# Sums of gated tiles beside the up rounds: from GpSimd to VectorE, one item ahead

## The chip, the cores and the metric

One NeuronCore of a Trainium2 chip runs the whole program. The metric is device time in microseconds, the median of several runs. TensorE multiplies, ScalarE (ACT), VectorE (DVE) and GpSimd (POOL) compute on tiles, and SyncE (SP) issues nearly all DMAs.

## What is computed

One layer of a hybrid encoder for 2048 prompt rows and 64 sample rows, 1024 wide: two token mixers, an output projection, and a gated feed-forward block with a short causal convolution. The change lies in the feed-forward block:

```python
h = modulate(x, norm_ffn_g[l], shift, scale)
up, cf_new = causal_dwconv(h @ ffn_up_w[l], cf_prev, ffn_conv_w[l], ffn_conv_b[l])
val, gt = jnp.split(up, 2, axis=-1)
x = x + gate[:, None, :] * ((val * jax.nn.gelu(gt)) @ ffn_down_w[l])
```

D_FF is 2816, so there are 22 tiles of 128 hidden channels (`NF`), in 11 pairs (`NI`).

## The kernel before

All engines run programs written out by hand, and semaphores tie them together. Nothing schedules: what stands first on an engine's queue runs first.

**Products with seven terms.** Each large matrix product is cut in 2 x 2 blocks and made from seven block products (Winograd's form of Strassen's scheme) in place of eight. That needs sums and differences of the blocks of both operands. Each operand, a block or a sum of blocks, is split in two f16 parts, high and low, and each product is three passes (high-high, high-low, low-high). ScalarE makes the high part by a copy, VectorE the low part by subtracting the high one.

**The up rounds.** Round f (1 to 21; round 0 stands ahead) multiplies all tokens by the up weights of hidden tile f. TensorE runs seven products `c` in three column groups `q` of 352, 21 blocks of 12 matmuls a round (L2981). ScalarE copies some of them out of PSUM (`copy`, L1751). VectorE combines others (`block`, L2635, L2638, L2641). `block(f, 1, 2)`, L2638 on the last 352 columns, is the last of them. ScalarE's `c21` (L1759 for the first two column groups, L1762 for the third) empties product 6. It stands on ScalarE's queue behind `first_tap(f, 0)` (L1788), which waits for that last `block`. TensorE's next round writes the banks that `c21` empties.

In round f VectorE also does the convolution of tile f - 1 (`ffn_conv`: L2651 and L2655, for the value and then for the gate half), the gated product of tile f - 1 (`product`, L2659), the sums of the next up weights (`weight_sums`, L2612 to L2617) and their low parts (`up_lo`, L2583). ScalarE makes the high parts (`up_hi`, L1713) and the gelu (L1794).

**Items.** The down product that comes after the up rounds needs the seven combinations of the gated hidden tiles as well. For the first eight pairs (`NQ` = 8) these are made beside the up rounds 3 to 18, in a loop of eight passes with two rounds each, `late` = 0 and 1. An item is 176 columns of one pair of tiles, six items a pair, so 48 items (`NITEM`), three a round. For an item, in this order:
- SP loads four blocks of 128x176 f32 from `ffn_hidden` (L942)
- four sums and differences are made in three new tiles and one of the loaded (`four_sums`, L1204 to L1209, on GpSimd)
- ScalarE makes the high parts (`item_hi`, L1810 and L1811)
- VectorE makes the low parts (`item_lo`, L2671 and L2673)
- SP stores all to `hidden_combinations` (L947)

Two sets of buffers for the loaded blocks and the sums are used in turns, one for the result.

**Units** are the same for the down weights: load (L932), four sums on GpSimd (`unit_sums`, L1194 to L1199), high parts (`unit_hi`, L1804, L1805), low parts (`unit_lo`, L2663, L2666), store (L936). There are two a round in the loop.

Where they stand in a round: `item_lo` of the first item behind the value half of the convolution, of the second behind `product`, of the third ahead of `up_lo` of weight 4. GpSimd's queue in a round holds sums of item, item, unit, item, unit. After the up rounds, `base_sums` on GpSimd does the same sums for the last three pairs.

SP's queue in a round: item store, item load, up weights, store of the hidden tile f - 1, item store, item load, unit store, unit load, item store, item load, unit store, unit load. Ahead of the loop it loads items 0 and 1.

Of the kernel before, what the change touches and what calls it, by code (L numbers as in the profile page):

```python
# [12 lines left out]
ALU = mybir.AluOpType  # L13
# [50 lines left out]
def build(nc, a):  # L64
    ctx = ExitStack()
    with ctx:
# [537 lines left out]
        LOAD_BASE = 8 * (NITEM + 2)  # L604
        SUM_BASE, HI_BASE, LO_BASE = 4 * NITEM, 2 * NITEM, 2 * NITEM + 6

# [516 lines left out]
        def _(pool):  # L1123
# [86 lines left out]

            def item_sums(n, i, u):
                pool.wait_ge(b_loaded[u % 2], 48 * i + 16 * (u // 2) + 16)
                pool.wait_ge(b_lo, 2 * n + 4)
                four_sums([itemr[u % 2][:, k] for k in range(4)], [isum[u % 2][:, k] for k in range(3)], 4 * n)

            def loop_sums(i, late):
                (n0, _, _), (n1, _, _), (n2, _, _) = loop_items(i, late)
                u0, u1 = loop_units(i, late)
                item_sums(n0, i, 3 * late)
                item_sums(n1, i, 3 * late + 1)  # L1220
                unit_sums(u0)
                item_sums(n2, i, 3 * late + 2)
                unit_sums(u1)
# [10 lines left out]

            def base_sums(s):
                if s == NB - 1:
                    pool.wait_ge(b_last, LAST_BASE + 16)
                else:
                    pool.wait_ge(b_loaded[s % 2], loads_done(s))
                if s >= 2:  # L1240
                    pool.wait_ge(b_lo, LO_BASE + 2 * (s - 1))
                four_sums([stage_of(s)[:, :, k] for k in range(4)], [dsum[s % 2][:, :, k] for k in range(3)],
                          SUM_BASE + 4 * s)
# [738 lines left out]
        def _(dve):  # L1982
# [678 lines left out]
            def unit_lo(n):  # L2661
# [5 lines left out]
                    .then_inc(wu_lo, 1)  # L2667

            def item_lo(n, i, u):
                dve.wait_ge(b_hi, 2 * n + 1)  # L2670
                dve.tensor_tensor(iout[:, 0:4, 1], itemr[u % 2], iout[:, 0:4, 0], ALU.subtract).then_inc(b_lo, 1)  # L2671
                dve.wait_ge(b_hi, 2 * n + 2)
                dve.tensor_tensor(iout[:, 4:7, 1], isum[u % 2], iout[:, 4:7, 0], ALU.subtract).then_inc(b_lo, 1)  # L2673

            def base_lo(s):
# [74 lines left out]
            ffn_round(1, units_of(1))  # L2750
            ffn_round(2, units_of(2))
            with nc.vector.Fori(0, LOOPS) as i:
                ffn_round(round_a(i), loop_units(i, 0), loop_items(i, 0))
                ffn_round(round_a(i) + 1, loop_units(i, 1), loop_items(i, 1))
# [589 lines left out]
```

## Time and profile before

| what | value |
|---|---|
| median of 3 runs | 2704.09 us (2703.27 to 2707.04) |
| the profiled execution | 2708.34 us, its span 2706.2 us |
| TensorE busy | 2645.6 us, 98% of the span |
| VectorE busy | 1750.4 us, 65% |
| ScalarE busy | 1361.6 us, 50% |
| GpSimd busy | 622.1 us, 23% |
| clock of TensorE that was granted | 0.993 of full speed |

The span is the time from the first to the last instruction of one execution. A row of a timeline gives the start and the length in us, the engine, the line, the operation with its output and input, the number of operations merged in it, and in brackets how long the engine stood idle before it and what ended that. An engine starts its next operation up to 0.1 us before the end that is shown of the one before, so the distance from start to start is what counts.

### The profile page before, as it was taken

What the parts mean: (1) busy time and instruction counts of PE and PEld (TensorE: products, weight loads), DVE (VectorE), ACT (ScalarE), POOL (GpSimd) and SP (SyncE); (2) the same over time, 40 slices, a digit from 0 to 9 for tenths busy, and PEclk for the clock granted to TensorE, in tenths of its full rate; (3) what the DMA queues carried; (4) which work ended last, traced back from release to release, by engine and by line L of the source; (5) the groups of instructions that cost most, each with busy time, mean ns of one, the idle gap of its engine ahead of it and who ended that gap; (6) DMA issues with size and microseconds to landing.
All of it is one profiled execution on the core that took longest, in us unless ns stands there. A gap on an engine that the chain in (4) does not pass through costs nothing.

```text
span 2706.2 us, 50623 instructions
## 1 busy us (share of the span) xinstructions
PE 2645.6 (98%) x18662; PEld 1771.9 (65%) x18662; DVE 1750.4 (65%) x3369; ACT 1361.6 (50%) x2666; POOL 622.1 (23%) x697
## 2 busy tenths in 40 slices
PE   8998999999999999999999999999999999999997
PEld 2465666666668888556997666666666666666664
DVE  4965374564746665767777788888888875242434
ACT  4966474655756665113556455565555653121211
POOL 2600000000008789000000245443344311101000
PEclk9999999999999999999999999999999999999999
DMA  8622212231183543456652354545545438566562
GB/s 280 201 71 98 102 62 71 70 111 69 62 234 96 123 143 126 174 215 189 149 142 64 125 183 167 182 163 184 181 159 182 164 122 327 206 238 253 221 249 91
DMA packets 238419, 423.07 MB, mean 156 GB/s; under 512 B 57816, under 2 KB 162776, under 8 KB 230056
## 3 DMA queue, kind: packets, MB, share of 16 engines
q1 hardware_dynamic: 229400, 412.03, 45.5%
q10 hardware_dynamic: 8848, 8.74, 0.9%
q8 instruction: 109, 1.79, 0.3%
q14 instruction: 62, 0.51, 0.1%
HBM read 283.42 MB, written 139.92 MB: 156 GB/s over the span
## 4 chain that ended last, share of the span: by engine, by line
PE 83%; DVE 5%; ACT 5%; DMA 2%; issue 2%; POOL 1%; SPq 1%; DVEq 0%; ACTq 0%; POOLq 0%
PE ps L2981 52%; PE ps L3228 14%; PE ps L3087 5%; PE ps L3073 4%; PE ps L3060 3%; PE ps L3049 2%; PE ps L2905 1%; ACT arena L1591 1%; DMA arena<-in_w_down 1%; PE ps L3022 1%; POOL arena L1137 1%; ACT arena L1598 1%; ACT arena L1272 1%; ACT arena L1306 1%; DMA gates<-arena 0%
## 5 line engine op out<-in xcount | busy, mean ns | idle before, releaser
L2981 PE MATMUL ps<-arena 128*128 128x352 f16 (+1 forms) x11880 | 1612.7, 298 | 6.2 <-ACT arena L1759 2.9
L2981 PEld LDWEIGHTS ps<-arena 128*128 128x128 f16 x11880 | 1102.2, 97 | 512.4 <-ACT arena L1759 3.6
L3228 PE MATMUL ps<-arena 128*128 128x352 f16 x2772 | 414.8, 311 | 0.5 <-DVE arena L2680 0.5
L3228 PEld LDWEIGHTS ps<-arena 128*128 128x128 f16 x2772 | 265.5, 96 | 149.9 <-issue 1.0
L1194 POOL TENSOR_TENSOR arena<-arena 128x128 f32<-128x128 f32 x44 | 30.7, 698 | 744.3 <-DMA arena<-in_w_down 744.2
L3087 PE MATMUL ps<-arena 128*128 128x424 f16 (+1 forms) x960 | 174.1, 343 | 3.4 <-DVE arena L2462 2.7
L1150 POOL CAST arena<-arena 64x512 f16<-64x512 f32 x8 | 4.9, 608 | 699.1 <-DMA arena<-in_cache_kT 698.9
L1751 ACT ACTIVATE arena<-ps 128x352 f32<-128x352 f32 x264 | 115.8, 459 | 95.0 <-PE ps L2981 95.0
L3073 PE MATMUL ps<-arena 128*128 128x64 f32 (+2 forms) x1200 | 148.8, 269 | 0.5 <-DVE arena L2426 0.5
L3087 PEld LDWEIGHTS ps<-arena 128*128 128x128 f16 x960 | 92.4, 97 | 84.8 <-DVE arena L2462 4.3
L1204 POOL TENSOR_TENSOR arena<-arena 128x176 f32<-128x176 f32 (+1 forms) x57 | 55.9, 981 | 399.6 <-DMA arena<-ffn_hidden 399.6
L3073 PEld LDWEIGHTS ps<-arena 128*128 128x128 f32 (+2 forms) x1200 | 142.5, 190 | 2.7 <-issue 0.8
L1389 ACT ACTIVATE arena<-ps 128x352 f32<-128x352 f32 x192 | 80.8, 462 | 122.1 <-PE ps L2981 122.1
L2783 DVE TENSOR_TENSOR arena<-ps,arena 128x352 f32<-128x352 f32 x12 | 6.3, 525 | 206.3 <-PE ps L3228 176.4
L2583 DVE SCALAR_TENSOR_TENSOR arena<-arena 128x512 f16<-128x512 f32 x154 | 104.7, 711 | 47.3 <-ACT arena L1713 47.3
L2651 DVE SCALAR_TENSOR_TENSOR arena<-arena 128x2114 f32<-128x2114 f32 x44 | 110.0, 2500 | 27.2 <-ACT arena L1788 27.2
L1598 ACT ACTIVATE arena<-ps 128x512 f32<-128x512 f32 (+3 forms) x136 | 76.2, 561 | 99.1 <-PE ps L3060 99.0
L1178 POOL TENSOR_TENSOR arena<-arena 128x1024 f32<-128x1024 f32 (+6 forms) x147 | 120.4, 819 | 13.6 <-POOL arena L1171 3.8
L2150 DVE SCALAR_TENSOR_TENSOR arena<-arena 128x512 f16<-128x512 f32 x112 | 73.9, 687 | 63.6 <-ACT arena L1368 63.4
L1944 ACT ACTIVATE arena<-ps 128x352 f32<-128x352 f32 x12 | 5.6, 463 | 205.7 <-PE ps L3228 205.7
L1788 ACT ACTIVATE arena<-arena 128x2114 f32<-128x2114 f32 x44 | 94.5, 2147 | 28.3 <-DVE arena L2638 27.3
L2655 DVE SCALAR_TENSOR_TENSOR arena<-arena 128x2114 f32<-128x2114 f32 x44 | 108.2, 2460 | 0.3
(236 smaller groups left out, 3580.1 us busy)
## 6 DMA issues: line engine op xcount, KB each, us to landing
hidden_combinations<-arena SPq DMA_DIRECT2D x48, 616.0 KB, 3.2
arena<-hidden_combinations SPq DMA_DIRECT2D x24, 1232.0 KB, 7.1
arena<-in_w_up SPq DMA_DIRECT2D x44, 512.0 KB, 4.8
down_combinations<-arena SPq DMA_DIRECT2D x44, 448.0 KB, 2.8
ffn_hidden<-arena SPq DMA_DIRECT2D x44, 440.0 KB, 3.1
arena<-down_combinations SPq DMA_DIRECT2D x10, 1792.0 KB, 7.7
arena<-down_combinations SPq DMA_DIRECT2D x20, 896.0 KB, 6.5
arena<-ffn_hidden SPq DMA_DIRECT2D x50, 352.0 KB, 3.9
```

The source lines that it names most:

```text
L1178: pool.tensor_tensor(out, djunk[:, :, 0:w], djunk[:, :, w:2 * w], ALU.add).then_inc(ada_step, 1)
L1598: act.activation(pt[:, x.h, 0:m * P], ps[:, 4, 0:m * P], ACT.Copy).then_inc(t_act, 1)
L1751: act.activation(fcp[(0, 1, 2, 0)[i]][q], ps[:, bank_of((0, 2, 3, 4)[i], q), 0:CF], ACT.Copy, scale=CSF)\
L1788: act.activation(out, u[:, 0:LF], ACT.Identity, scale=w0, bias=fb).then_inc(f_tap, 1)
L2583: dve.scalar_tensor_tensor(fsp[:, c, :, 1, :], src.rearrange("p (k m) -> p k m", k=4), -WSF if c == 6 else WSF, fsp[:, c, :, 0, :], ALU.mu ...
L2651: dve.scalar_tensor_tensor(out, u[:, 1:1 + LF], tap(1), out, ALU.mult, ALU.add).then_inc(f_conv, 1)
L2655: dve.scalar_tensor_tensor(out, u[:, 2:2 + LF], tap(2), out, ALU.mult, ALU.add).then_inc(f_conv, 1)
L2981: mm = pe.matmul(out, wt[:, k, wp, :], act_t[:, k, hp], start=(first and k == 0 and n == 0), stop=(last and k == K - 1 and n == 2), skip_g ...
L3060: mm = pe.transpose(ps[0:k, 4 + c // 4, (c % 4) * P:(c % 4) * P + x.rows], pr[0:x.rows, x.h, c * P:c * P + k], ident[0:x.rows, 0:x.rows])
L3073: mm = pe.matmul(ps[0:x.rows, 6, 64 * x.h:64 * x.h + 64], pt[0:k, x.h, c * P:c * P + x.rows], vv[x.b][0:k, x.v0 + c, 64 * x.h:64 * x.h + 6 ...
L3087: mm = pe.matmul(out, wt[:, wp, k, :], mixT[:, k, hp, t:t + w], start=(k == k0 and m == 0), stop=(k == k1 - 1 and m == 2))
L3228: mm = pe.matmul(ps[:, down_bank(n, k), 0:CF].rearrange("p (w t) -> p w t", w=2), dwt(i)[:, wi, wp, :], dact[i][:, :, bi, hp, :], start=(i ...
```

## The change

The four sums of an item are taken off GpSimd's queue and made by VectorE, with the same semaphore `b_sum`. VectorE makes the sums of item n + 1 directly behind `item_lo` of item n, and those of item 0 ahead of the loop. The last pass makes one set that nobody uses (item 48, for which a load stood there already), so the later counts of `b_sum` grow by four. GpSimd keeps the unit sums and `base_sums`.

```diff
-        SUM_BASE, HI_BASE, LO_BASE = 4 * NITEM, 2 * NITEM, 2 * NITEM + 6
+        SUM_BASE, HI_BASE, LO_BASE = 4 * NITEM + 4, 2 * NITEM, 2 * NITEM + 6
...
-            def item_sums(n, i, u):
-                pool.wait_ge(b_loaded[u % 2], 48 * i + 16 * (u // 2) + 16)
-                pool.wait_ge(b_lo, 2 * n + 4)
-                four_sums([itemr[u % 2][:, k] for k in range(4)], [isum[u % 2][:, k] for k in range(3)], 4 * n)
-
             def loop_sums(i, late):
-                (n0, _, _), (n1, _, _), (n2, _, _) = loop_items(i, late)
                 u0, u1 = loop_units(i, late)
-                item_sums(n0, i, 3 * late)
-                item_sums(n1, i, 3 * late + 1)
                 unit_sums(u0)
-                item_sums(n2, i, 3 * late + 2)
                 unit_sums(u1)
...
             def base_sums(s):
+                if s == 0:
+                    pool.wait_ge(b_sum, SUM_BASE)
...
+            def four_sums(blocks, sums, at0):
+                b12, b11, b22, b21 = blocks
+                t0, t2, t3 = sums
+                dve.tensor_tensor(t0, b12, b11, ALU.subtract).then_inc(b_sum, 1)
+                dve.wait_ge(b_sum, at0 + 1)
+                dve.tensor_tensor(b12, b22, b12, ALU.subtract).then_inc(b_sum, 1)
+                dve.tensor_tensor(t2, b22, t0, ALU.subtract).then_inc(b_sum, 1)
+                dve.wait_ge(b_sum, at0 + 3)
+                dve.tensor_tensor(t3, b21, t2, ALU.subtract).then_inc(b_sum, 1)
+
+            def item_sums(n, i, u):
+                dve.wait_ge(b_loaded[u % 2], 48 * i + 16 * (u // 2) + 16)
+                dve.wait_ge(b_lo, 2 * n + 4)
+                four_sums([itemr[u % 2][:, k] for k in range(4)], [isum[u % 2][:, k] for k in range(3)], 4 * n)
+
             def item_lo(n, i, u):
...
                 dve.tensor_tensor(iout[:, 4:7, 1], isum[u % 2], iout[:, 4:7, 0], ALU.subtract).then_inc(b_lo, 1)
+                item_sums(n + 1, i + (u + 1) // 6, (u + 1) % 6)
...
             ffn_round(2, units_of(2))
+            item_sums(0, 0, 0)
             with nc.vector.Fori(0, LOOPS) as i:
```

The functions moved down by some lines, so the same operation has another line number after: L2663 and L2666 (unit low parts) are L2656 and L2659, L2651 is L2644, L2671 and L2673 are L2679 and L2681.

VectorE's queue at the entrance of the loop, before. The unit's low parts end round 2, and the convolution opens round 3:

```order
L2663 SCALAR_TENSOR_TENSOR arena<-arena 128x4x128 [waits wu_hi]
L2666 SCALAR_TENSOR_TENSOR arena<-arena 128x3x128 [waits wu_hi]
L2752 UNCONDITIONAL_BRANCH
L2752 ISA
L2651 ISA [waits f_tap]
L2651 SCALAR_TENSOR_TENSOR arena<-arena 128x2114
```

The same place after:

```order
L2656 SCALAR_TENSOR_TENSOR arena<-arena 128x4x128 [waits wu_hi]
L2659 SCALAR_TENSOR_TENSOR arena<-arena 128x3x128 [waits wu_hi]
L2665 TENSOR_TENSOR arena<-arena 128x176 [waits b_lo,b_loaded0]
L2667 TENSOR_TENSOR arena<-arena 128x176 [waits b_sum]
L2668 TENSOR_TENSOR arena<-arena 128x176
L2670 TENSOR_TENSOR arena<-arena 128x176 [waits b_sum]
L2762 UNCONDITIONAL_BRANCH
L2762 ISA
L2644 ISA [waits f_tap]
L2644 SCALAR_TENSOR_TENSOR arena<-arena 128x2114
```

The sums of item 0, with their wait for the load, stand ahead of the loop and of the convolution now.

VectorE's queue in round 3 behind the first item's low parts, before, up to the low part of the up weights (L2583):

```order
L2670 ISA
L2671 TENSOR_TENSOR arena<-arena 128x4x176 [waits b_hi]
L2672 REGISTER_ALU
L2673 TENSOR_TENSOR arena<-arena 128x3x176 [waits b_hi]
L2582 ISA
L2583 SCALAR_TENSOR_TENSOR arena<-arena 128x4x128 [waits p_hi]
```

The same place after:

```order
L2678 ISA
L2679 TENSOR_TENSOR arena<-arena 128x4x176 [waits b_hi]
L2680 REGISTER_ALU
L2681 TENSOR_TENSOR arena<-arena 128x3x176 [waits b_hi]
L2673 ISA
L2674 ISA [waits b_loaded1]
L2665 TENSOR_TENSOR arena<-arena 128x176 [waits b_lo]
```

Between the low parts of an item and the next work of the round stand a wait for the next item's load and four operations. The other two items of a round have the same piece.

## Rows read from the trace of the kernel before

**Rows 1.** The page: busy time of the engines; DMA issues, count, size, us to landing.
```profile
PE 2645.6 (98%) x18662; PEld 1771.9 (65%) x18662; DVE 1750.4 (65%) x3369; ACT 1361.6 (50%) x2666; POOL 622.1 (23%) x697
...
arena<-ffn_hidden SPq DMA_DIRECT2D x50, 352.0 KB, 3.9
```

**Rows 2.** Timeline of TensorE, the up rounds: start, length, line, count, idle before.
```profile
1519.27 75.36 PE L2981 MATMUL ps<-arena 128*128 128x352 f16 x504 [2.14 <-ACT arena L1759]
1595.34 676.79 PE L2981 MATMUL ps<-arena 128*128 128x352 f16 x4536 [0.71 <-ACT arena L1759]
```

**Rows 3.** Timeline of all engines, one steady round, 1824 to 1857 us.
```profile
1825.39 0.89 DVE L2671 TENSOR_TENSOR arena<-arena 128x704 f16<-128x704 f32 x1 [1.18 <-ACT arena L1810]
...
1830.60 2.42 DVE L2655 SCALAR_TENSOR_TENSOR arena<-arena 128x2114 f32<-128x2114 f32 x1
...
1835.14 2.36 DVE L2659 SCALAR_TENSOR_TENSOR arena<-arena 128x2114 f32<-128x2114 f32 x1 [0.42 <-ACT arena L1794]
...
1843.16 0.35 SPq L942 DMA_DIRECT2D arena<-ffn_hidden  x1
...
1845.45 0.69 DVE L2583 SCALAR_TENSOR_TENSOR arena<-arena 128x512 f16<-128x512 f32 x1 [0.99 <-ACT arena L1713]
...
1849.03 0.69 DVE L2583 SCALAR_TENSOR_TENSOR arena<-arena 128x512 f16<-128x512 f32 x1 [1.39 <-ACT arena L1713]
...
1851.52 0.52 DVE L2638 SCALAR_TENSOR_TENSOR arena<-ps,arena 128x352 f32<-128x352 f32 x1 [0.23 <-PE ps L2981]
...
1853.31 0.59 DVE L2638 SCALAR_TENSOR_TENSOR arena<-ps,arena 128x320 f32<-128x320 f32 x2 [0.38 <-PE ps L2981]
...
1854.16 2.15 ACT L1788 ACTIVATE arena<-arena 128x2114 f32<-128x2114 f32 x1 [1.48 <-DVE arena L2638]
...
1856.21 0.44 ACT L1759 ACTIVATE arena<-ps 128x352 f32<-128x352 f32 x1
```

**Rows 4.** Groups by line and shape, 1595 to 2150 us: count | busy us, mean ns | idle before.
```profile
L1204 POOL TENSOR_TENSOR arena<-arena 128x176 f32<-128x176 f32 x44 | 42.8, 973 | 92.0 <-DMA arena<-ffn_hidden 92.0
...
L1207 POOL TENSOR_TENSOR arena<-arena 128x176 f32<-128x176 f32 x44 | 26.3, 598 | 0.0
```

**Rows 5.** Timeline of VectorE, a chain of three dependent operations ahead of the up rounds.
```profile
1425.63 0.53 DVE L2540 TENSOR_TENSOR arena<-arena 128x352 f32<-128x352 f32 x1
1426.19 0.34 DVE L2542 TENSOR_TENSOR arena<-arena 128x176 f32<-128x176 f32 x1
1426.45 0.52 DVE L2530 SCALAR_TENSOR_TENSOR arena<-ps,arena 128x144 f32<-128x144 f32 x2
```

**Rows 6.** Timeline of all engines, round 3, the first of the loop, 1555 to 1596 us.
```profile
1555.97 2.42 DVE L2651 SCALAR_TENSOR_TENSOR arena<-arena 128x2114 f32<-128x2114 f32 x1 [1.43 <-ACT arena L1788]
...
1559.78 1.60 POOL L1204 TENSOR_TENSOR arena<-arena 128x176 f32<-128x176 f32 x1 [7.16 <-DMA arena<-ffn_hidden]
...
1564.03 1.05 DVE L2671 TENSOR_TENSOR arena<-arena 128x704 f16<-128x704 f32 x1 [3.06 <-ACT arena L1810]
...
1570.62 2.41 DVE L2655 SCALAR_TENSOR_TENSOR arena<-arena 128x2114 f32<-128x2114 f32 x1
...
1575.15 2.71 DVE L2659 SCALAR_TENSOR_TENSOR arena<-arena 128x2114 f32<-128x2114 f32 x1 [0.43 <-ACT arena L1794]
1575.22 0.44 ACT L1751 ACTIVATE arena<-ps 128x352 f32<-128x352 f32 x1
...
1586.68 0.89 DVE L2671 TENSOR_TENSOR arena<-arena 128x704 f16<-128x704 f32 x1 [1.25 <-ACT arena L1810]
...
1588.43 0.69 DVE L2583 SCALAR_TENSOR_TENSOR arena<-arena 128x512 f16<-128x512 f32 x1 [0.24 <-ACT arena L1713]
...
1591.79 0.58 DVE L2638 SCALAR_TENSOR_TENSOR arena<-ps,arena 128x320 f32<-128x320 f32 x2
...
1592.80 2.13 ACT L1788 ACTIVATE arena<-arena 128x2114 f32<-128x2114 f32 x1
...
1594.84 0.79 ACT L1759 ACTIVATE arena<-ps 128x352 f32<-128x352 f32 x2
```

## The prediction

> **What bounds the kernel now.** I read first the table of engines: TensorE is busy for 98% of the span [rows 1]. So a change on other engines can only cost or give back time where TensorE waits. The second view is therefore TensorE's own timeline through the up rounds [rows 2]. It has two waits there. One is 2.14 us at 1519.27, before round 2 and ahead of the changed loop. The other is 0.71 us at 1595.34, at the start of round 4. After it stand 4536 matmuls in one piece of 676.79 us, 18 rounds of 37.6 us, with no wait at all. Both waits were ended by L1759 on ScalarE. That is `c21`, which empties the first bank of a round's last product. TensorE's next round writes the same bank. So this is the link that ends last, and the question is how near it is to being late in the other rounds.
>
> The third view is one steady round [rows 3]. Round 11 begins on TensorE at 1595.34 + 7 x 37.6 = 1858.5, round 10 at 1820.9. Read the chain ahead of the boundary at 1858.5 backwards: L1759 on ScalarE starts at 1856.21 and ends at 1856.65. It follows the first tap (L1788, 1854.16, 2.15 us), which waited 1.48 us for VectorE's last block (L2638, 1853.31, two pieces, 0.59 us). That block had itself waited 0.38 us for TensorE. The bank is free at 1856.65 and wanted at 1858.47: **a margin of 1.82 us in each round**. VectorE may reach its last block 1.8 us late, and TensorE sees nothing.
>
> **The change, part by part.** GpSimd loses four TENSOR_TENSORs per item, 48 items. Its rows run from 973 ns (L1204) to 598 ns (L1207) for the same shape [rows 4]. Nobody on the path waited for them in the steady rounds: the unit sums that remain on GpSimd wait for a DMA, not for the item sums. So the removal itself gives TensorE nothing.
>
> VectorE gains the four, once per item, behind that item's low halves and for the item after it. Price: the same shape on VectorE is L2542, 128x176 f32, 0.34 us [rows 5]. Where it waits for the operation before it, it starts 0.03 us after that one's end (1425.63 + 0.53 to 1426.19). Where nothing binds the next one, that starts 0.26 us after it (1426.19 to 1426.45). Of the four, two wait for a sum before them. So an item costs 0.37 + 0.26 + 0.37 + 0.26 = **1.26 us**, and three items a round 3.78 us. The bounds: 4 x 0.26 = 1.04 us if no wait is felt, and GpSimd's own price, at least 4 x 0.60 = 2.4 us, if the waits and register instructions cost there what they cost on GpSimd. I take 1.26, as engine and shape are those of the row.
>
> The Trainium skill, "VectorE: DVE Perf Modes", section on the TRN2 errata, gives (N+151)/0.96 ns for such an operation, an estimate of 341 ns that the row bears out, and advises tiles of 512 elements or more, since a small one pays the fixed part alone. By it four serial operations are 1.36 us, and the lateness below would be 1.1 in place of 0.8 us.
>
> In the **steady rounds** the 3.78 us fall between the item's low halves at 1825.39, which ScalarE paces (VectorE waited 1.18 us for it there), and the last block at 1853.31. On that way VectorE waited 0.99 us (1845.45), 1.39 (1849.03), 0.23 (1851.52) and 0.38 (1853.31): 2.99 us that added work can fill. The waits of 0.42 us and less behind a gelu or its own conv stay, since they move with the work. The last block comes 3.78 - 2.99 = **0.79 us late**, the margin falls from 1.82 to about 1.0 us, and TensorE still doesn't wait. The lateness doesn't grow from round to round, for at the next round's item VectorE has another wait for ScalarE (1.18 us at 1825.39) that takes it up. Relief from GpSimd's absence on top is small here, so I count none.
>
> Two waits are new on VectorE. Sums of the item after next wait for its load (`b_loaded`). Behind that wait stand the split of weight 4, the blocks and the last block, and for these wait ScalarE and TensorE. The latest load is issued at 1843.16 [rows 3] and takes 3.9 us [rows 1], so it lands at 1847.1, and some 1.3 us later once the product before it has moved. VectorE was through with the low halves before it at 1849.03 - 1.39 = 1847.64, and would come to it at 1847.64 + 2 x 1.26 - 0.99 = 1849.2. The load lands 0.8 us ahead of need, and a miss of up to 1.0 us is still inside the margin. The wait on `b_lo` is on VectorE's own work of two items back.
>
> At the **entrance of the loop** there is no such cover. VectorE now makes the sums of item 0 ahead of round 3, and the load lands for GpSimd only at 1559.78 [rows 6]. GpSimd waited 7.16 us for it. VectorE had begun its first conv at 1555.97. Now everything behind the sums on VectorE's queue waits with them. Step by step, as lateness against before:
> - first conv: 1559.78 + 1.26 - 1555.97 = +5.07
> - low halves of item 0: the 3.06 us wait at 1564.03 is filled: +2.01
> - second conv, second half (1570.62): one item's sums (+1.26). But VectorE took 6.59 us from 1564.03 to there with GpSimd beside it, against 5.21 in the steady round (1825.39 to 1830.60), so 1.38 come back: +1.89
> - product: 2.71 us before against 2.36 in steady rounds: its end +1.54
> - one more item: +2.80; the wait of 1.25 at 1586.68 is filled, and ScalarE behind the later store is 1.54 late itself: +1.55
> - one more item +2.81, the wait of 0.24 at 1588.43 filled: +2.57 at the last block (1591.79)
> - the first tap on ScalarE began 0.43 us after the block's end, against 0.26 in the steady round, so 0.17 are absorbed: **+2.4** for L1759 and so for TensorE, which was waiting for it already.
>
> Round 4 so begins at 1597.7 in place of 1595.34. Inside round 3 the nearest other need is ScalarE's copy at 1575.22, ending 1575.66. TensorE wants it at 1595.34 - 0.71 - 37.6 + 12 x 1.79 = 1578.5 (twelve of 21 blocks), and +1.9 leaves 0.9 us. From round 4 on the tap ends 0.4 us before the boundary, a conv of 4.9 us later is 4.5 us behind it, and 1825.39 is also 4.5 us behind its boundary: the steady state holds at once.
>
> **The Trainium skill speaks of a lock.** The rows first: beside GpSimd the stretch of 5.21 us took 6.59. "SBUF — State Buffer", section on the two separate sides, says that VectorE and GpSimd share a port pair, and that the one who comes second "fully blocks". By it the relief could be larger than what I counted. What that gives is the second rival.
>
> **Sum.** The profiled execution took 2708.34 us, 4.25 above the median of the three runs. I go by differences: nothing removed from TensorE's path, +2.4 us at one boundary, nothing in the 15 rounds behind it, nothing after the loop, where the operations are the same. 2704.09 + 2.4 = **2706.5 us**.
>
> **Rivals.**
> 1. *VectorE overruns every round (slower).* The margin of 1.82 is crossed when three items cost over 2.99 + 1.82 = 4.81 us, 1.60 us an item. At 2.0 us an item, between my price and GpSimd's 2.4, each boundary is 3 x 0.40 = 1.2 us late, times 15 boundaries 18 us, and the entrance 2.4 + 4 x 0.74 = 5.4: 2727 us. For it: two more waits per item and their register instructions, which no row of VectorE shows in a row of four. Against it: the 0.03 us at the dependent operation. 0.11.
> 2. *Nothing is lost, or the 0.71 us comes back.* If item 0 is absorbed by relief from GpSimd, the wait at 1595.34 goes at most: 2703.4 us. It needs 3.1 us more relief than the rows show. This is also the outcome if the port lock rule above holds for every operation of round 3. 0.10.
> 3. *Two stalls at the entrance.* If the first load is 1 us later (landings spread), round 3 itself stops at the copy, and the total is 3 to 6 us: 2708 to 2710. 0.12, inside the range.
> 4. *A true gain.* TensorE waits 0.71 us in the whole of the changed loop, so over 5.4 us can't come from it. 0.02.
>
> **How the numbers follow.** The forecast gets 0.65. The bounds of its price, 1.04 and about 1.6 us an item, put four items at the entrance at -0.9 and +1.4 us, so it covers 2705.5 to 2708. With the second and third rival and the 3.8 us by which runs of the kernel before differ, the range is 2702.5 to 2710.5, and the first rival is left out. Around 0.2%, 5.4 us, is what a measurement can tell from no change here: faster 0.02, within 0.86, slower 0.12.
>
> **What the profile after would show.** TensorE's timeline has its wait at the start of round 4 grown from 0.7 to about 3 us, and one piece of 18 rounds of 37.6 us behind it. VectorE's first sum waits some 5 us for `ffn_hidden` before round 3. In steady rounds the waits of 0.99 and 1.39 us ahead of the weight splits of product 3 and 4 are gone or nearly so, and L1759 ends 0.8 us nearer to the boundary. A sum of 176 columns takes 0.34 us. I am wrong if TensorE waits for ScalarE or VectorE at more than one boundary, if an item takes over 1.6 us, or if the sums wait for a load in steady rounds by over 1 us.

## The result, and the profile after

The changed kernel took 2716.36 us (median of 7 runs, 2710.93 to 2718.64), the kernel before 2708.01 us (7 runs, 2703.27 to 2712.43). The ratio is 1.0025, 95% interval [1.0014, 1.0036]: slower, and outside the predicted range. Run again later (the first experiment), the same kernel stood at 1.0014 [1.0004, 1.0023]. Neither interval holds 1, and the two ratios put the loss at 6.8 and 3.8 us.

The page after: the engines, and the up products (line, matmuls, busy us and mean ns, idle us before them with the releaser). They answer [rows 1].

```profile
PE 2649.7 (98%) x18662; PEld 1772.7 (65%) x18662; DVE 1793.0 (66%) x3565; ACT 1360.5 (50%) x2666; POOL 481.2 (18%) x505
...
L2991 PE MATMUL ps<-arena 128*128 128x352 f16 (+1 forms) x11880 | 1613.9, 298 | 10.4 <-ACT arena L1752 7.2
```

Work went from GpSimd (141 us less) to VectorE (43 us more, for 196 instructions). TensorE has the same 18662 matmuls, and 7.2 us of its idle time were ended by L1752. That is `c21`, L1759 before. Other lines have moved too: L1781 is the first tap (L1788), L1803 the high half of an item (L1810), L2576 `up_lo` (L2583), L2631 the last `block` (L2638), L2652 `product` (L2659), L2665 to L2670 the sums, now on VectorE.

TensorE's timeline after, the up rounds, against [rows 2]:

```profile
1520.94 75.35 PE L2991 MATMUL ps<-arena 128*128 128x352 f16 x504 [2.08 <-ACT arena L1752]
1601.38 678.31 PE L2991 MATMUL ps<-arena 128*128 128x352 f16 x4536 [5.09 <-ACT arena L1752]
2279.53 31.50 PE L3238 MATMUL ps<-arena 128*128 128x352 f16 x210
```

The whole difference can be read here. The wait at round 4 has grown from 0.71 to 5.09 us. The 4536 matmuls behind it are in one piece again, with no wait at any of the 17 later boundaries, but the piece is 1.52 us longer (678.31 against 676.79). The two windows of TensorE behind that wait say why (window, its length, TensorE busy, granted clock as a share of full speed):

```profile
1601.40:1604.80 3.40, 3.40 (x13) 0.54 0.40 120
1604.80:1638.00 33.20, 33.20 (x225) 1.00 0.52 176
```

In the first window behind the 5.09 us wait TensorE ran at 0.54 of full speed, that is mostly at its lower level, 1.2 GHz, and in the second at 2.4 GHz again. In the profile before, no such stretch follows the 0.71 us wait.

**The measure used from here on.** The time of a whole run can't carry a difference of 3 us from one profile. In the twelve profiles of this study, round 2 of the up rounds starts anywhere from 1517.62 to 1530.06 us, and no kernel changes anything ahead of it. So I take the distance from the start of round 2 to the first down product, which holds all that the change touches in the up rounds. (Behind it the two kernels took 434.2 and 434.4 us.) Before it is 752.70 us (1519.27 to 2271.97, which is where the piece of [rows 2] is followed by the down product). After it is 2279.53 - 1520.94 = 758.59 us: 5.89 us more, 4.37 for the later start of round 4 and 1.52 for the clock. The spans differ by 7.7 us (2713.9 against 2706.2); 1.67 us of that lie ahead of round 2.

**A steady round after**, round 10, against [rows 3]. Its end on TensorE is 1601.38 + 1.52 + 7 x 37.6 = 1866.1.

```profile
1830.03 2.66 POOL L1196 TENSOR_TENSOR arena<-arena 128x128 f32<-128x128 f32 x1
...
1832.96 0.89 DVE L2679 TENSOR_TENSOR arena<-arena 128x704 f16<-128x704 f32 x1 [0.59 <-ACT arena L1803]
...
1852.26 0.35 SPq L942 DMA_DIRECT2D arena<-ffn_hidden  x1
...
1856.74 0.34 DVE L2665 TENSOR_TENSOR arena<-arena 128x176 f32<-128x176 f32 x1
...
1858.26 0.96 DVE L2576 SCALAR_TENSOR_TENSOR arena<-arena 128x512 f16<-128x512 f32 x1
...
1861.64 0.58 DVE L2631 SCALAR_TENSOR_TENSOR arena<-ps,arena 128x320 f32<-128x320 f32 x2
...
1862.47 2.15 ACT L1781 ACTIVATE arena<-arena 128x2114 f32<-128x2114 f32 x1 [1.17 <-DVE arena L2631]
...
1864.53 0.80 ACT L1752 ACTIVATE arena<-ps 128x352 f32<-128x352 f32 x2
```

VectorE's waits of 0.99, 1.39, 0.23 and 0.38 us ahead of its last block are gone. The bank is free at 1864.53 + 0.44 = 1864.97 and wanted at 1866.1, a margin of 1.1 us, where it was 1.82. A load issued at 1852.26 is used at 1856.74, and VectorE doesn't wait for it. The price of a sum, by groups of line and shape from 1602 to 2150 us (count | busy us, mean ns | idle before):

```profile
L2670 DVE TENSOR_TENSOR arena<-arena 128x176 f32<-128x176 f32 x44 | 17.5, 398 | 1.5
...
L2665 DVE TENSOR_TENSOR arena<-arena 128x176 f32<-128x176 f32 x44 | 14.9, 339 | 0.0
```

**The entrance of the loop after**, round 3, against [rows 6]:

```profile
1561.14 0.57 DVE L2665 TENSOR_TENSOR arena<-arena 128x176 f32<-128x176 f32 x1 [5.22 <-DMA arena<-ffn_hidden]
...
1562.74 2.42 DVE L2644 SCALAR_TENSOR_TENSOR arena<-arena 128x2114 f32<-128x2114 f32 x1
...
1567.66 0.89 DVE L2679 TENSOR_TENSOR arena<-arena 128x704 f16<-128x704 f32 x1
...
1574.12 2.42 DVE L2648 SCALAR_TENSOR_TENSOR arena<-arena 128x2114 f32<-128x2114 f32 x1
...
1578.67 2.36 DVE L2652 SCALAR_TENSOR_TENSOR arena<-arena 128x2114 f32<-128x2114 f32 x1 [0.42 <-ACT arena L1787]
...
1586.06 0.33 SPq L947 DMA_DIRECT2D hidden_combinations<-arena  x1
...
1590.65 0.79 ACT L1803 ACTIVATE arena<-arena 128x704 f16<-128x704 f32 x1 [3.48 <-DMA hidden_combinations<-arena]
...
1591.47 0.89 DVE L2679 TENSOR_TENSOR arena<-arena 128x704 f16<-128x704 f32 x1 [1.63 <-ACT arena L1803]
...
1592.90 0.34 DVE L2665 TENSOR_TENSOR arena<-arena 128x176 f32<-128x176 f32 x1
...
1593.25 0.45 POOL L1194 TENSOR_TENSOR arena<-arena 128x128 f32<-128x128 f32 x1 [31.73 <-DMA arena<-in_w_down]
1593.27 0.63 DVE L2667 TENSOR_TENSOR arena<-arena 128x176 f32<-128x176 f32 x1
...
1594.87 0.96 DVE L2576 SCALAR_TENSOR_TENSOR arena<-arena 128x512 f16<-128x512 f32 x1
...
1597.99 0.58 DVE L2631 SCALAR_TENSOR_TENSOR arena<-ps,arena 128x320 f32<-128x320 f32 x2
...
1600.88 0.80 ACT L1752 ACTIVATE arena<-ps 128x352 f32<-128x352 f32 x2
```

Read it from the top. VectorE stands 5.22 us for the load of item 0 with the convolution behind it. It makes that up in part by the third row, the low halves of item 0, since a wait for ScalarE that stood there before (3.06 us) is filled. From 1586.06 on a second loss appears. The store of item 1 is issued there, and only when it has landed may ScalarE overwrite the result tile with item 2 (1590.65). VectorE waits for that, and then makes the next sums while GpSimd makes its unit sums.

### The profile page after: what moved, and what is told of

Its sections match the earlier page's. It is cut to its first block, busy times and chain, and to the rows that moved or that the text cites. A ratio compares the mean times of both kernels' runs of the same rounds, so it can differ in the third digit from the quotient of the medians.

```text
span 2713.9 us, 50637 instructions
## 1 busy us (share of the span) xinstructions
PE 2649.7 (98%) x18662; PEld 1772.7 (65%) x18662; DVE 1793.0 (66%) x3565; ACT 1360.5 (50%) x2666; POOL 481.2 (18%) x505
## 4 chain that ended last, share of the span: by engine, by line
PE 82%; DVE 5%; ACT 5%; DMA 3%; issue 2%; POOL 1%; SPq 1%; DVEq 0%; ACTq 0%; POOLq 0%
PE ps L2991 52%; PE ps L3238 14%; PE ps L3097 4%; PE ps L3083 4%; PE ps L3070 3%; PE ps L3059 2%; PE ps L2915 1%; ACT arena L1584 1%; PE ps L3032 1%; DMA arena<-in_w_down 1%; POOL arena L1137 1%; ACT arena L1265 1%; ACT arena L1591 1%; ACT arena L1299 1%; DMA gates<-arena 0%
## 5 line engine op out<-in xcount | busy, mean ns | idle before, releaser
L1194 POOL TENSOR_TENSOR arena<-arena 128x128 f32<-128x128 f32 x44 | 23.3, 529 | 997.6 <-DMA arena<-in_w_down 997.6
L2644 DVE SCALAR_TENSOR_TENSOR arena<-arena 128x2114 f32<-128x2114 f32 x44 | 107.0, 2431 | 32.9 <-ACT arena L1781 32.9
L1787 ACT ACTIVATE arena<-arena 128x1057 f32<-128x1057 f32 x44 | 45.3, 1076 | 146.7 <-DVE arena L2648 146.7
L2576 DVE SCALAR_TENSOR_TENSOR arena<-arena 128x512 f16<-128x512 f32 x154 | 105.7, 726 | 14.5 <-ACT arena L1706 14.5
L1781 ACT ACTIVATE arena<-arena 128x2114 f32<-128x2114 f32 x44 | 94.5, 2147 | 22.4 <-DVE arena L2631 22.1
```

What stands on the lines that cost most here:

```text
L1781: act.activation(out, u[:, 0:LF], ACT.Identity, scale=w0, bias=fb).then_inc(f_tap, 1)
L2576: dve.scalar_tensor_tensor(fsp[:, c, :, 1, :], src.rearrange("p (k m) -> p k m", k=4), -WSF if c == 6 else WSF, fsp[:, c, :, 0, :], ALU.mu ...
L2644: dve.scalar_tensor_tensor(out, u[:, 1:1 + LF], tap(1), out, ALU.mult, ALU.add).then_inc(f_conv, 1)
```

## The experiments

Three theories stood against each other. (1) The entrance: VectorE starts round 3 some 5 us late behind the load of item 0, TensorE waits for that at round 4 and gets a lower clock for a moment behind the wait. (2) Chance: a long landing of a store, or of the clock, in one execution. (3) Steady overload: VectorE has more to do in each round than it can hide.

The first four ran on one chip and share one set of runs of the kernel before (33 runs, median 2709.98 us); the next four share another (25 runs, 2710.64), the last two a third (23 runs, 2710.84); these six ran on one chip too, another one. "Late" means: counted from the start of round 2, later than the same operation of the kernel before.

**The changed kernel again.** No edit.

> The changed kernel once more, on the chip of the variants below. Theory 1 (entrance): TensorE's timeline again has one long wait in the loop, 4 to 5.5 us at the start of round 4, its clock at half for the first 10 or so matmuls behind it, and 18 rounds of 37.59 us; time over the kernel before by 5 to 7 us. Theory 2 (the long landing of the store in round 3, 4.5 us against 3.2 us before, was chance): the wait is 3 to 4 us this time and the time 3 to 5 us over. Theory 3 (steady overload): waits at several boundaries.

Measured: 2712.0 us (2709.82 to 2716.82), ratio 1.0014 [1.0004, 1.0023]. TensorE's timeline:

```profile
1518.46 77.03 PE L2991 MATMUL ps<-arena 128*128 128x352 f16 x504 [2.09 <-ACT arena L1752]
1597.80 676.79 PE L2991 MATMUL ps<-arena 128*128 128x352 f16 x4536 [2.30 <-ACT arena L1752]
2274.43 55.82 PE L3238 MATMUL ps<-arena 128*128 128x352 f16 x373
```

755.97 us from round 2 to the down product, 3.27 more than before. The lower clock came here at the start of round 2 (504 matmuls in 77.03 us against 75.36). TensorE loses nothing by it directly, since round 4 must wait for `c21` anyway: 0.71 + 3.27 - 1.68 = 2.30, the wait that stands there. The wait came out shorter than either theory had it, and the 3.27 us, like the 3.8 us of the ratio, are what was expected of theory 2. So the loss at the entrance is a mark of the kernel, and its size varies. The long landing of the store and the clock behind the wait belong to the first profile: the store of item 1 landed in 3.5 us here, against 4.5 us there. The entrance itself was later here, though. The load of item 0 was issued 36.70 us after the start of round 2, against 35.92 us in the first profile. Whether the lower clock in round 2 did that is not shown.

**Item 0 alone back on GpSimd**, the other 47 on VectorE:

```diff
+            pool.wait_ge(b_loaded[0], 16)
+            pool.wait_ge(b_lo, 4)
+            four_sums([itemr[0][:, k] for k in range(4)], [isum[0][:, k] for k in range(3)], 0)
             with nc.gpsimd.Fori(0, LOOPS) as i:
...
-            item_sums(0, 0, 0)
             with nc.vector.Fori(0, LOOPS) as i:
```

> The changed kernel, but the sums of item 0 alone are made by GpSimd ahead of the loop, so VectorE waits for no load before round 3; it still makes the other 47 items' sums and one more. Theory 1 (the entrance makes the loss): the first conv of round 3 starts where it did in the kernel before, the wait at round 4 is 0.7 to 2 us, the clock stays full behind it, time 0 to 2 us over the kernel before. Theory 3 (VectorE's load in each round makes the loss): the wait at round 4 may shrink, but the time stays 5 us or more over the kernel before.

Measured: 2712.42 us, ratio 1.0007 [0.9997, 1.0016].

```profile
1525.56 77.03 PE L2993 MATMUL ps<-arena 128*128 128x352 f16 x504 [2.01 <-ACT arena L1755]
1602.85 676.79 PE L2993 MATMUL ps<-arena 128*128 128x352 f16 x4536 [0.27 <-ACT arena L1755]
```

The wait at round 4 is 0.27 us, and 753.92 us pass to the down product (at 2279.48). The lower clock at round 2 makes TensorE 1.67 us later there, and the wait at round 4 is 0.44 us shorter than before: 752.70 + 1.67 - 0.44 = 753.93. Two readings fit this sum. `c21` comes 1.2 us later than before (1602.36 against 1594.84, with round 2 at 1525.56 against 1519.27), so some of these 1.2 us may be the price of the other items at the entrance, hidden here behind the clock, and some of it the clock's. The first convolution of round 3 is 0.4 us late already, ahead of any sum on VectorE. What the run shows is that item 0 makes the greater part of the loss (3.27 or 5.89 us with it), and that the other 47 leave at most 1.2 us. The runs with the loads behind unit 5, below, settle the rest. In whole runs the difference to the changed kernel, 0.0007, is smaller than the intervals; the reading rests on the timeline.

**Both loads earlier, in the changed kernel and in the kernel before.** SP issues the loads of items 0 and 1 in round 2, directly behind the stores of hidden tile 1:

```diff
                     if n == units_of(f)[0]:
                         store_hidden(f - 1)
+                        if f == 2:
+                            item_load(0, 0, 0)
+                            item_load(1, 0, 1)
...
-            item_load(0, 0, 0)
-            item_load(1, 0, 1)
             with nc.sync.Fori(0, LOOPS) as i:
```

> The changed kernel, but SyncE issues the loads of items 0 and 1 in round 2 right behind the store of hidden tile 1, some 7 us earlier, so the data are there when VectorE comes to the sums of item 0. VectorE still makes all sums. Theory 1: VectorE's wait of 5 us is gone, the first conv starts within 0.5 us of the kernel before, low halves of item 0 start 2 us earlier than in the kernel before, and the wait at round 4 is 0 to 0.7 us: time 0 to 1 us below the kernel before. Theory 3: 3 us or more above it.

> The kernel before with the same early loads of items 0 and 1. GpSimd makes the sums of items 0 and 1 while VectorE ends round 2, so VectorE's wait of 3.06 us for the high halves of item 0 falls to about 0.6 us and round 3 ends earlier: the wait of 0.71 us at round 4 goes, time 0.7 us below the kernel before, which this measurement can't tell from none. If it is the same as e2, where the sums are made doesn't matter once the load is early.

Measured: 2711.53 us, 1.0006 [0.9996, 1.0016] with the sums on VectorE, and 2709.83 us, 1.0005 [0.9996, 1.0014] with GpSimd's. To the down product 754.16 and 754.06 us, 1.7 us of each the lower clock behind the wait at round 2. The loads landed 10 us sooner, and the two kernels agree within 0.1 us, so the early load takes the difference between them away. But the gain that was expected on top did not come: the first convolution of round 3 was not back in its place. In the first of them, on GpSimd:

```profile
1560.42 0.45 POOL L1195 TENSOR_TENSOR arena<-arena 128x128 f32<-128x128 f32 x1 [8.02 <-DMA arena<-in_w_down]
```

The item loads wait for the landing of the hidden tile's store. SP stands there, and the unit's store and load are queued behind. ScalarE's first tap, which stands behind the unit's high parts, came 2.1 us later in the one and 2.5 us in the other than in the two runs above. I put that down to SP standing still, but this is the smaller part. The load of unit 5 was issued only 0.6 us later than with item 0 on GpSimd (28.60 us after the start of round 2, against 27.97). What made the difference is its landing, behind two item loads of 352 KB issued just ahead. DMA issues for a window around it, here and in the next version, where it goes ahead of them:

```profile
arena<-in_w_down SPq DMA_DIRECT2D x1, 256.0 KB, 5.3
```

```profile
arena<-in_w_down SPq DMA_DIRECT2D x1, 256.0 KB, 3.1
```

It took 5.7 us in the kernel before with the early loads, and 3.1 us with item 0 on GpSimd.

**Loads behind the load of unit 5.** The same edit, but one unit later in round 2, so that the load of unit 5 goes ahead of the item loads (the store of unit 5 and the load of unit 6 follow them):

```diff
                         unit_load(n + 1)
+                    if f == 2 and n == units_of(f)[1]:
+                        item_load(0, 0, 0)
+                        item_load(1, 0, 1)
```

> The changed kernel with the loads of items 0 and 1 issued in round 2 behind the load of unit 5, so behind the store of hidden tile 1 but without SyncE standing still for its landing ahead of a unit's store and load (in the run with the loads right behind the store, ScalarE's first tap of round 2 came 2 us late through that). Theory 1 (the load at the entrance makes the loss): the tap is back in its place, the first conv of round 3 starts within 0.5 us of the kernel before, TensorE's wait at round 4 is under 0.5 us, and from the start of round 2 to the first down product it takes 752 us plus 1.7 us where the clock is at half in round 2; time -1 to +0.5 us against the kernel before. Theory 3 (VectorE's load in each round): 3 us or more over it.

Measured: 2709.19 us (2703.25 to 2714.6), ratio 0.9989 [0.9977, 1.0000]. VectorE first, then TensorE:

```profile
1555.15 0.33 DVE L2666 TENSOR_TENSOR arena<-arena 128x176 f32<-128x176 f32 x1
...
1556.66 2.42 DVE L2645 SCALAR_TENSOR_TENSOR arena<-arena 128x2114 f32<-128x2114 f32 x1 [0.17 <-ACT arena L1782]
```

```profile
1520.34 751.97 PE L2992 MATMUL ps<-arena 128*128 128x352 f16 x5040 [2.05 <-ACT arena L1753]
2272.15 31.50 PE L3239 MATMUL ps<-arena 128*128 128x352 f16 x210
```

The sums of item 0 find their data, and the convolution waits 0.17 us for ScalarE, no longer for the sums. The two pieces of TensorE have become one of 5040 matmuls. 751.81 us to the down product: all 5.9 us of the loss in the first profile are gone, and the 0.9 us that the kernel before loses at round 4 as well. `c21` starts at 1593.83 ahead of round 4 in this version and is 1.3 us early (1593.83 + 0.44 against 1520.34 + 2 x 37.6 = 1595.5).

**Work in place of the wait.** On that version, 14 dependent operations of 176 columns behind the sums of item 0, to keep VectorE from the convolution as long as the load did:

```diff
             item_sums(0, 0, 0)
+            more_work(14, 0)
```

with `more_work(k, before)` doing k times a wait for VectorE's own last operation and `dve.tensor_tensor(spare, par[:, 0:HW], par[:, HW:2 * HW], ALU.subtract)`.

> The same with the loads in time, but 14 operations of 128x176 on spare columns, each waiting for the one before it (14 x 0.37 = 5.2 us), behind the sums of item 0 on VectorE; work added, result unchanged. Theory 1: a busy VectorE costs as much as one that waits, so the first conv of round 3 is about 5 us late again and the wait at round 4 is 2 to 4.5 us. If instead the loss came from the loads and stores around the loop's first items being later or slower, the wait stays under 1 us here. Time 2 to 6 us over the kernel before.

Measured: 2714.16 us, ratio 1.0013 [1.0000, 1.0025].

```profile
1519.32 75.36 PE L3000 MATMUL ps<-arena 128*128 128x352 f16 x504 [2.05 <-ACT arena L1753]
1598.78 678.47 PE L3000 MATMUL ps<-arena 128*128 128x352 f16 x4536 [4.11 <-ACT arena L1753]
2277.08 31.50 PE L3247 MATMUL ps<-arena 128*128 128x352 f16 x210
```

The 14 operations took 5.83 us, the wait at round 4 is back (4.11 us), with a longer piece behind it (678.47), and 757.76 us pass. The convolution of round 3 starts 5.6 us late here and `c21` comes 3.4 us late. What matters is that the convolution starts some 5 us late, not that a DMA is the reason.

**One and three more operations per item.** On the version with the loads behind the unit, to find how much more VectorE could take in each round: `more_work(1, 1 * n)` and `more_work(3, 3 * n)` behind the four sums in `item_sums`, 3 and 9 a round at 0.37 us each by the price above.

> The loads in time, and one more operation of 128x176 (0.37 us) on VectorE behind each item's sums, three a round. The prediction put the margin of L1759 before a round's start at 1.0 us with the sums in place; the trace shows 1.1. Expected: the last block another 1.1 us later, margin 0 to 0.1 us, so a wait of 0 to 0.1 us a round; time 0 to 2 us over the kernel before. If the margin were softer than read (VectorE would overlap more), no change at all; if VectorE had no margin, 1.1 us a round, 17 us.

> Three more such operations behind each item's sums, 3 x 3 x 0.37 = 3.3 us a round. By the margin of 1.1 us TensorE waits 3.3 - 1.1 = 2.2 us a round once the lateness has built up, less what other waits take up, over 15 rounds: 25 to 40 us over the kernel before, with one wait at the start of each round. If VectorE's queue is as full as that, its busy share in the loop comes to over 95% and the wait is what exceeds the round. A sign against: no waits at most boundaries.

Measured: 2721.99 us, ratio 1.0036 [1.0020, 1.0051], and 2756.25 us, 1.0174 [1.0150, 1.0198]. Both are above what was expected: 11 us over the kernel before by the medians where 0 to 2 were, and 46 where 25 to 40 were. TensorE with three more operations a round:

```profile
1524.42 112.94 PE L3000 MATMUL ps<-arena 128*128 128x352 f16 x756 [1.95 <-ACT arena L1753]
1637.98 37.76 PE L3000 MATMUL ps<-arena 128*128 128x352 f16 x252 [0.62 <-ACT arena L1753]
1676.44 37.76 PE L3000 MATMUL ps<-arena 128*128 128x352 f16 x252 [0.70 <-ACT arena L1753]
```

and ScalarE's `c21` in the same run, at the ends of rounds 2, 3 and 4:

```profile
1560.56 0.80 ACT L1753 ACTIVATE arena<-ps 128x352 f32<-128x352 f32 x2
...
1599.01 0.80 ACT L1753 ACTIVATE arena<-ps 128x352 f32<-128x352 f32 x2
...
1637.48 0.80 ACT L1753 ACTIVATE arena<-ps 128x352 f32<-128x352 f32 x2
```

The steady overload of theory 3 is thus possible, but not at the price of the change. More is to be read here. By the margin at the boundary (1.1 us), 3 x 0.37 = 1.11 us should just fit, or miss once by little. But `c21` comes every 38.46 us where TensorE needs 37.6. At the first boundary it is 1.0 us early (1561.00 against 1524.42 + 37.6 = 1562.0), at the second 0.2, at the third too late, and from there on each round takes 38.2 to 38.5 us. **The lateness adds up from round to round**, until TensorE waits. VectorE and ScalarE have a cycle of their own. Without the added 1.11 us it would be some 37.35 us; from the other run, where `c21` comes every 40.54 us with 3.33 us added, 37.2. By that price VectorE would have 0.2 to 0.4 us left in a round. The added operations cost more than the price, however. From the start of an item's sums to the next work, VectorE took 1.31 us on average in the changed kernel (1640 to 2150 us), and 1.75 and 2.64 us in these two runs, so 1.3 and 4.0 us a round were added. By these figures 0.5 and 1.0 us were left. So the estimate from the two runs is 0.2 to 1.0 us. That the lateness adds up is shown; that what is left is far below the margin of 1.1 us is not. The other figure that was expected, VectorE busy for over 95% of the loop, didn't come either. From 1640 to 2150 us it was busy for 84.6% before, 91.4% after, and 93.7% and 93.5% with more work, although TensorE waited in nearly every round.

With nine more operations a round, TensorE's waits and pieces mostly alternate:

```profile
1677.17 39.28 PE L3000 MATMUL ps<-arena 128*128 128x352 f16 x252 [2.80 <-ACT arena L1753]
1717.68 37.76 PE L3000 MATMUL ps<-arena 128*128 128x352 f16 x252 [1.23 <-ACT arena L1753]
```

A piece that ran at the lower clock at first (0.55 of full speed in the first 3.4 us of the piece at 1677.17) is 1.4 to 1.7 us longer, and the wait behind it is shorter by as much, for the period is set by `c21`. A lower clock costs time only where TensorE doesn't wait afterwards, as in the 18 rounds behind round 4's start.

**The early load without the change, beside the best version again.** The kernel before with its loads behind the load of unit 5, and the changed kernel with them:

> The kernel before (sums of the items on GpSimd), with the first two item loads issued inside round 2 behind unit 5's load. It asks whether the gain of the last version lies in the earlier load or in the place of the sums. If the entrance is all that stands between the kernels (theory 1), TensorE runs from the start of round 2 to the first down product in 751.8 us as there (752.7 before), with no wait ahead of round 4, and the time is that of the version with VectorE's sums within 1 us. If the larger margin of the kernel before in the steady rounds (1.8 us against 1.1) were worth something (theory 3), it would be over 1 us faster than that version.

> The changed kernel with the two loads behind unit 5's load once more, beside the same load order with GpSimd's sums, on one chip. Expected by theory 1: no wait ahead of round 4, 751.8 us from the start of round 2 to the first down product, and 0.999 of the time before. Should the 5 us of the entrance have been luck of one execution (theory 2), the wait ahead of round 4 comes back here at 1 to 5 us.

Measured: 2710.45 us, ratio 0.9996 [0.9983, 1.0009], and 2709.15 us, 0.9997 [0.9985, 1.0009]. TensorE in the one and the other:

```profile
1526.72 751.97 PE L2982 MATMUL ps<-arena 128*128 128x352 f16 x5040 [2.02 <-ACT arena L1760]
2278.53 31.50 PE L3229 MATMUL ps<-arena 128*128 128x352 f16 x210
```

```profile
1519.87 751.97 PE L2992 MATMUL ps<-arena 128*128 128x352 f16 x5040 [2.08 <-ACT arena L1753]
2271.68 128.50 PE L3239 MATMUL ps<-arena 128*128 128x352 f16 x860
```

751.81 us in both. With the load in time it doesn't matter to TensorE who makes the sums. Both versions do better than the changed kernel in the trace. Against the kernel before their 0.9 us in the trace is real, but whole runs (0.9989, 0.9997 and 0.9996, each interval touching or holding 1) can't show it.

## Why the prediction was wrong, point by point

**What bounds the kernel, and that it can only lose at TensorE's waits:** right. All of the 5.89 us lie at the one boundary that was named, and behind it.

**Price and steady rounds:** right in the numbers; one reason given for them is not (see rival 1 below). An item starts its four sums 0.37, 0.26, 0.37 and 0.26 us apart, 1.26 us as forecast from [rows 5], except where GpSimd works beside; with these the mean is 1.31 us. (The third of [rows 5] is free of the two before it, against that group's heading, and the prediction reads it so.) The last block came 0.7 us late (0.79 forecast), the margin was 1.1 us (1.0), no wait for a load, no wait of TensorE at 17 boundaries. By the Trainium skill's formula ("VectorE: DVE Perf Modes", section on the TRN2 errata) four would have been 1.36 us. The records of 0.34 us agree with that figure, the distances from start to start don't, since an independent one follows after 0.26 us.

**The entrance, as steps of lateness in us.** The counting is that of the experiments; the last column is the changed kernel's second profile.

| step | forecast | after | after again |
|---|---|---|---|
| first conv | +5.07 | +5.10 | +5.83 |
| low halves of item 0 | +2.01 | +1.96 | +2.69 |
| second conv, second half | +1.89 | +1.83 | +2.56 |
| end of product | +1.54 | +1.49 | +2.22 |
| low halves of item 2 | +1.55 | **+3.12** | +2.49 |
| `up_lo` of weight 4 | +2.57 | **+4.77** | +3.42 |
| last block | +2.57 | +4.53 | +3.42 |
| `c21` | +2.4 | +4.37 | +3.27 |

Four steps hold within 0.06 us. For the first of them that is in part luck: VectorE's first sum started 0.31 us earlier than GpSimd's had (40.20 us after the start of round 2 against 40.51), and the sums of item 0 took 1.60 us in place of 1.26. **The fifth is the one that failed.** I had ScalarE behind the later store "1.54 late itself". The store was issued 1.85 us late (1586.06 - 1520.94 = 65.12, against 1582.54 - 1519.27 = 63.27 in the trace before), because SP had been held up on its way too, and took longer to land. The page of DMA issues for a window around it, after and before:

```profile
hidden_combinations<-arena SPq DMA_DIRECT2D x1, 616.0 KB, 4.5
```

```profile
hidden_combinations<-arena SPq DMA_DIRECT2D x1, 616.0 KB, 3.2
```

That is 0.3 and 1.3 us, 1.6 together. I had moved the store and left its length as it was, and gave no range to a transfer on the path. In the second profile it took 3.5 us, and the low halves of item 2 were 0.6 us less late than in the first, although everything ahead of them was 0.7 us later. Whether the long landing was chance or the company of the hidden tile's stores (one of them took 1.12 us to issue, where it took 0.38 before) is open. One run speaks for chance: with work in place of the wait, one of these stores took 0.95 us to issue, and the store of item 1 landed in 3.5 us.

**The sixth step was mis-sized as well.** The sums of the next item took 1592.90 to 1594.87 = 1.97 us where 1.26 were priced, since GpSimd's unit sums (1593.25) fell beside them: 0.63, 0.61 and 0.48 us for operations of 0.34. The split behind them lost another 0.27 us, and the blocks behind it gave 0.5 back. I had argued that GpSimd would be relieved. It was, but the shift moved VectorE's sums into the unit sums that remain. In the second profile the unit sums fell behind the sums, and those took 1.26 us. There the first step is the one that was mis-sized: it stands 0.76 us higher than forecast, half of it because the first sum started 0.38 us later than in the kernel before, half because the sums of item 0 took 1.64 us. With that in place of +5.07 the rest of the chain comes out within 0.2 us of the forecast. So the mechanism of the chain was right, and the sizes of single terms were taken as fixed that vary from one execution to the next. 2.4 us was too little in each of the three profiles with the late entrance: 4.37, 3.27 and, with work in place of the wait, 3.39.

**A term that was not in the sum: the clock behind the wait.** 1.52 us, with TensorE mostly at 1.2 GHz (0.54) in the first 3.4 us behind 5.09 us of idleness. It is no fixed price: after 0.71 us it didn't happen, after some 2.1 us at round 2 it came in the four profiles on the first chip of the experiments, and in none of the other eight.

**The Trainium skill's lock** ("SBUF — State Buffer", section on the two separate sides) was weighed as a reason for a smaller loss, the second rival, 2703.4 us. That rival fell. The trace does agree with the rule itself where the two engines meet: in the steady round above, the unit sum of GpSimd at 1830.03, which runs beside a 2.41 us convolution, takes 2.66 us, and the next of its shape 0.45 (1832.64). The relief that I counted for the first half of round 3 was right within 0.01 us (1567.66 to 1574.12 is 6.46 us, 5.21 + 1.26 forecast). It wasn't larger.

**The base.** I added to the three-run median of 2704.09 us. Over seven runs the kernel before stands at 2708.01, and over 23 to 33 runs in the later comparisons at 2710 to 2711. So 3.9 of the 9.9 us of the miss are the base, and 6.0 the difference, 8.35 between the medians in place of 2.4. In the profiled execution 2.0 of these are the chain of the entrance (4.37 for 2.4), 1.5 the clock, 1.7 lie ahead of the up rounds and are not the change's; the rest is spread. The profiled execution of before, 2708.34 us, was the better base of the two that I had.

**The range and the chances.** A range of 4 us to each side was as wide as three runs of one kernel, without the base's own error. The chance of slower, 0.12, stood on a steady overload and left out that the entrance itself could pass 5.4 us. Rival 3, a second stall at the entrance worth 3 to 6 us, had the right size and place. But its mechanism, round 3 stopping at ScalarE's copy, didn't occur. Of the three signs of being wrong that the prediction names none came, for all three look for a loss in the steady rounds or for a dear item, and the loss was at the entrance.

**Rival 1's threshold is neither confirmed nor refuted.** I let it begin at 1.60 us an item, where the boundary's margin is used up. With one more operation an item took 1.75 us in the trace, and each round became 0.8 to 0.9 us too long, where the threshold gives 3 x 0.15 = 0.45. With three more it took 2.64 us, and each round became 2.9 us too long, where it gives 3.1. What these runs do refute is a reason given for the steady rounds. The wait of 1.18 us at [rows 3] does not stop the lateness from growing. It belongs to the same cycle, because what ScalarE does there stands on its queue behind the tap that waits for VectorE's last block. At the price of the change nothing hung on that.

## What to carry to other kernels

Before a step is put on a queue ahead of a loop, look when its data land in the first pass: in the steady rounds a load may be early by design, and at the entrance it is not. The same edit with the load issued earlier cost nothing, provided the early load did not stand just ahead of another load that the path needed. And how much more an engine can take per round can't be read off the margin at the boundary alone: shift everything by the added work, follow the chain once around to its own start, and see whether the wait there is one that shifts along.

## What the runs showed of the hardware

- TensorE's clock behind a short wait: after 5.09 and 4.11 us of idleness it fell to 0.5 of full speed for a few us (0.54 and 0.66 over the first 3.4 us), 1.5 and 1.7 us lost. After 3.18 and 2.70 us it didn't in one run, after 2.80 us it did in the same run, and after 2.0 to 2.1 us in the four profiles on one chip and not in those on the other. So the length of the wait alone doesn't decide it.
- VectorE beside GpSimd: an operation of 0.34 us takes 0.48 to 0.63 us, one of 0.69 takes 0.96. Behind a long VectorE operation GpSimd waits for all of it (2.66 us for 0.45).
- A 256 KB load on SP's queue landed in 5.3 and 5.7 us behind two loads of 352 KB issued just ahead, and in 3.1 us without them. The same 616 KB store took 3.2, 3.5 and 4.5 us in three executions.
- The same kernels reached round 2 anywhere within 12.4 us (1517.62 to 1530.06), with nothing changed ahead of it. A change of 3 us is seen in the distance between two matmuls, and not in the total.
